# The end of the mixers in another order: one score level moved first, one branch's matmuls moved between the outputs of the linear attention, the output projection by halves of k

## The reference, cut to what matters

```
h = rms_norm(x);  proj = h @ w_in          # queries, keys, values of four mixers, and 4096 gate columns
y_nsa, y_sb, y_fox, y_gla                  # four mixers, 512 columns each; y_gla is the linear attention
branch = einsum('bsnc,ncd->bsnd', ys, w_branch)        # 4 products of 512 by 1024
mixed  = sum over n of sigmoid(gate_logits + b_gate)[n] * branch[n]
x = x + mixed @ w_out                      # 1024 by 1024
h2 = rms_norm(x);  x = x + relu(h2 @ w_ff1)**2 @ w_ff2
```

## Time and profile before

| | us |
|---|---|
| median of 3 runs | 1999.48 (1998.98 to 1999.66) |
| the profiled execution, its own time | 1997.83 |
| its span, first to last instruction | 1996.0 |
| PE busy | 1784.7 (89%) |
| DVE busy | 855.8 (43%) |
| ACT busy | 691.7 (35%) |
| POOL busy | 106.7 (5%) |
| mean granted TensorE clock | 0.950 |

### The profile page before, as it was taken

How to read it: one execution, slowest core, us unless ns; L and a number is a source line. 1 busy time by engine, 2 the same in 40 slices (tenths; PEclk the granted TensorE clock), 3 DMA queues, 4 the chain that set the end, 5 groups by cost and what they waited for, 6 DMA issues and landing times.

```text
span 1996.0 us, 27472 instructions
## 1 busy us (share of the span) xinstructions
PE 1784.7 (89%) x11676; PEld 1410.7 (71%) x11676; DVE 855.8 (43%) x1435; ACT 691.7 (35%) x1042; POOL 106.7 (5%) x112
## 2 busy tenths in 40 slices
PE   6987598899998869999997979998999989779997
PEld 4864443344443369889897879887889989769985
DVE  3033411111111154633476757535543446765643
ACT  1230211111111135654445334324555444534431
POOL 0000000000000001400200000000230110000000
PEclk9988699999999979999998989998999999889998
DMA  5422299999999845332422434534532333343451
GB/s 238 178 109 95 88 422 427 430 427 429 427 429 429 359 170 211 127 126 99 156 99 113 169 126 170 199 146 176 203 123 109 114 123 135 120 168 127 169 219 74
DMA packets 30872, 412.22 MB, mean 207 GB/s; under 512 B 3600, under 2 KB 5040, under 8 KB 5808
## 3 DMA queue, kind: packets, MB, share of 16 engines
q1 hardware_dynamic: 30768, 410.70, 51.5%
HBM read 408.85 MB, written 1.84 MB: 206 GB/s over the span
## 4 chain that ended last, share of the span: by engine, by line
PE 70%; issue 12%; DMA 9%; DVE 5%; ACT 2%; POOL 1%; SPq 0%; DVEq 0%; POOLq 0%; ACTq 0%
PE bank L1068 9%; PE bank L1069 9%; PE bank L1073 9%; DMA work_mem<-in_w 8%; PE bank L986 8%; PE bank L750 3%; PE bank L758 3%; PE bank L1003 3%; PE bank L1080 2%; PE bank L1081 2%; PE bank L1082 2%; PE bank L1090 2%; PE bank L1095 2%; PE bank L1091 2%; PE bank L1365 1%
## 5 line engine op out<-in xcount | busy, mean ns | idle before, releaser
L2190 DVE TENSOR_TENSOR w_lo<-wring,w_hi 128x2048 fp32r<-128x2048 f32 x88 | 201.3, 2292 | 186.4 <-ACT w_hi L1597 186.4
L1597 ACT ACTIVATE w_hi<-wring 128x2048 fp32r<-128x2048 f32 x88 | 168.6, 1916 | 301.8 <-PE bank L1069 168.3
L1068 PE MATMUL bank<-mixed_hi,w_hi_early 128*128 128x256 f32 x960 | 246.0, 293 | 7.0 <-DVE mixed_lo L2198 4.8
L1069 PE MATMUL bank<-mixed_lo,w_hi_early 128*128 128x256 f32 x960 | 240.5, 287 | 0.0
L1597 ACT ACTIVATE w_hi_early<-wring 128x2048 fp32r<-128x2048 f32 x80 | 152.9, 1911 | 231.5 <-PE bank L1069 154.5
L2190 DVE TENSOR_TENSOR w_lo<-wring,w_hi_early 128x2048 fp32r<-128x2048 f32 x80 | 182.5, 2286 | 90.1 <-ACT w_hi_early L1597 89.9
L1073 PE MATMUL bank<-mixed_hi,w_lo 128*128 128x256 f32 x1472 | 208.4, 285 | 0.0
L1068 PEld LDWEIGHTS bank<-mixed_hi,w_hi_early 128*128 128x128 f32 x960 | 187.8, 196 | 13.2 <-issue 8.1
L1073 PEld LDWEIGHTS bank<-mixed_hi,w_lo 128*128 128x128 f32 x1472 | 192.1, 194 | 0.0
L1069 PEld LDWEIGHTS bank<-mixed_lo,w_hi_early 128*128 128x128 f32 x960 | 188.2, 196 | 0.1
L986 PE MATMUL bank<-wring,gates_mem 128*64 128x512 f32 x768 | 168.3, 594 | 12.5 <-DMA wring<-in_w 12.5
(11 more groups left out here) (418 smaller groups left out, 3044.2 us busy)
## 6 DMA issues: line engine op xcount, KB each, us to landing
wring<-in_w SPq DMA_DIRECT2D x160, 2048.0 KB, 8.6
work_mem<-in_w SPq DMA_DIRECT2D x32, 2048.0 KB, 17.1
cst<-in_const SPq DMA_DIRECT2D x1, 1288.0 KB, 7.6
prm<-in_prm SPq DMA_DIRECT2D x3, 381.0 KB, 8.2
x_mem<-in_x SPq DMA_DIRECT2D x1, 1024.0 KB, 4.9
out_x<-x_mem SPq DMA_DIRECT2D x1, 1024.0 KB, 3.9
rel_skew<-work_mem SPq DMA_DIRECT2D x1, 768.0 KB, 3.6
work_mem<-in_prm SPq DMA_DIRECT2D x1, 512.0 KB, 12.6
```

The lines of the kernel that those rows point to most:

```text
L1068: pe.matmul(out, w[0][:, k, cols], x[0][:, k, :], start=(k == 0), stop=False)
L1069: mm = pe.matmul(out, w[0][:, k, cols], x[1][:, k, :], start=False, stop=False)
L1597: act.activation(hi, w, ACT.Copy).then_inc(hi_ready, 1)
L2190: dve.tensor_tensor(lo, w, hi, ALU.subtract).then_inc(lo_ready, 1)
```

## The change, and the diff

- **Levels.** `gla_steps` gives level 8 first, then 0 to 7, with the same eight gate products between. DVE reads level 8 in the step of level 0.
- **Halves.** The two-buffer part goes on for two halves more (`RINGED = LATE + 2`), so both halves of the first mixer's branch weight use `w_hi_early`.
- **ACT.** The sigmoid of the gate and `y_high(0)` move ahead of gate product 15, `y_high(1)` and `y_high(2)` follow level 7, and the gate sigmoids 0 to 3 are spread otherwise.
- **DVE.** `y_low(0)` moves ahead of the last level's reading, `y_low(1)` behind `var8`, `y_low(2)` behind `y_gla`, and the first four gated products are spread between them (`gated`).
- **PE.** The first branch's first product comes before `gla_o`, its other three between `gla_o` and `gla_t`; the banks follow (`plan_layer`).
- **Output projection.** All four column and row blocks with k tiles 0 to 3 first, then those with 4 to 7. The halves come as (26, first), (27, first), (26, second), (27, second) (`OUT_HALVES`). SP's table `uses` is not changed: chunk 26 is given free by `out` product 1, chunk 27 by `out` product 3.

```
+RINGED = LATE + 2
+OUT_HALVES = [(26, 0), (27, 0), (26, 1), (27, 1)]
...
-    for n in range(len(GLA_LEVELS) + 1):
+    for n in [levels] + list(range(levels)):
...
-    for name, count in (("gla_o", 2), ("gla_t", 2), ("branch", 16), ...
+    for name, count in (("branch", 1), ("gla_o", 2), ("branch", 3), ("gla_t", 2), ("branch", 12), ...
...
+        if 26 <= c < 28:
+            c, second = OUT_HALVES[h - (LATE + 8)]
...
 PE
+            branch(0, [0])
             in_sbuf(layer["gla_v"] + [j for n in range(9) for j in layer["gla", "level", n]], l, layer["gla_o"][0])
             for i, j in enumerate(layer["gla_o"]):
...
+            branch(0, [1, 2, 3])
             pe.wait_ge(y_gla, l + 1)
             for i, j in enumerate(layer["gla_t"]):
                 turn_four(j, o_g[:, i, :], l)
-            for n in range(N_BRANCH):
-                branch(n)
+            for br in range(1, N_BRANCH):
+                branch(br, range(4))
             for h in range(4):
-                half, second = divmod(h, 2)
+                second, half = divmod(h, 2)
                 w = half_ready(LATE + 8 + h)
-                pe.wait_ge(mixed_ready, 4 * l + (2 if h == 0 else 4))
+                pe.wait_ge(mixed_ready, 4 * l + (2 if second == 0 else 4))
...
 ACT
-                if h % 2 == 0:
+                if h % 2 == 0 or h == LATE + 9:
                     act.wait_ge(w_landed[c % RING], layer_landed(c, l))
...
+                elif n < last:
                     level(n + 1)
+                    if n == last - 1:
+                        act.activation(flat(sig_gg), flat(g_g), ACT.Sigmoid).then_inc(g_sig, 1)
+                        act.wait_ge(level_ready, 8 * l + last + 1)
+                        y_high(0)
+            full(layer["gla", "level", last][-1], l)
+            y_high(1)
+            y_high(2)
...
+            gate_sigmoid(0)
             (squares and copies of gla_o)
+            split_hi(RINGED + 0)
+            gate_sigmoid(1)
             act.wait_ge(var8_ready, l + 3)
+            split_hi(RINGED + 1)
+            gate_sigmoid(2)
             act.wait_ge(y_gla, l + 1)
+            split_hi(RINGED + 2)
...
 DVE
+            y_low(0)
+            level_read(levels - 1)
+            split_lo(LATE + 1)
             (silu and gain, sum of squares, var8)
+            y_low(1)
+            gated(0)
             dve.wait_ge(rstd8_ready, l + 3)
             then(dve.tensor_tensor(heads8(o_g), heads8(o_g), by_head(rstd8), ALU.mult))
             dve.tensor_tensor(o_g, o_g, sig_gg, ALU.mult).then_inc(y_gla, 1)
+            split_lo(RINGED + 0)
+            gated(1)
+            y_low(2)
+            gated(2)
+            split_lo(RINGED + 1)
+            gated(3)
             (low part of gla_t)
+            split_lo(RINGED + 2)
+            for n in range(4, 4 * N_BRANCH):
+                if n % 2 == 0:
+                    split_lo(LATE + n // 2 + AHEAD)
+                gated(n)
```

More of the change, by code:

```diff
@@ L340, in plan_layer @@
                 r.add((mixer, kind, n))
-    for name, count in (("gla_o", 2), ("gla_t", 2), ("branch", 16), ("out", 4), ("h2", 4), ("ff1", 16), ("ff2", 4)):
+    for name, count in (("branch", 1), ("gla_o", 2), ("branch", 3), ("gla_t", 2), ("branch", 12), ("out", 4), ("h2", 4), ("ff1", 16), ("ff2", 4)):
         r.add(name, count)
@@ L1368, in _, with branch @@
                                 mm.then_inc(bank_full[j.bank], 1)
+            def branch(br, ks):
+                pe.wait_ge(y_lo_ready, 5 * l + (br + 1 if br < 3 else 5))
+                tiles = slice(4 * br, 4 * br + 4)
+                for k in ks:
+                    w = half_ready(LATE + 2 * br + k // 2)
+                    split_a(layer["branch"][4 * br + k], w, 256 * (k % 2), (y_hi[:, tiles, :], y_lo[:, tiles, :]), k % 2 == 1)
+            branch(0, [0])
             in_sbuf(layer["gla_v"] + [j for n in range(9) for j in layer["gla", "level", n]], l, layer["gla_o"][0])
@@ L1591, in split_hi @@
                 c, w, hi, lo = weight_half(h)
-                if h % 2 == 0:
+                if h % 2 == 0 or h == LATE + 9:
                     act.wait_ge(w_landed[c % RING], layer_landed(c, l))
-                ahead, first = (2, 0) if h < LATE else (AHEAD, LATE)
+                ahead, first = (2, 0) if h < RINGED else (AHEAD, RINGED)
                 if h - first >= ahead:
@@ L1612, in next_hi @@
             def next_hi(h):
[L1613 removed]
+                if h + 2 < RINGED:
                     split_hi(h + 2)
@@ L1752, in _ @@
                     fill(*n)
-                else:
+                elif n < last:
                     level(n + 1)
-            for j in last_in_bank(layer["gla_g"] + layer["gates"]):
-                act.wait_ge(bank_read[j.bank], j.count(l))
[L1757 to L1764, removed]
+                    if n == last - 1:
+                        for j in last_in_bank(layer["gla_g"]):
+                            act.wait_ge(bank_read[j.bank], j.count(l))
+                        act.activation(flat(sig_gg), flat(g_g), ACT.Sigmoid).then_inc(g_sig, 1)
[4 more added lines that the diff above has]
+            y_high(2)
+            for j in last_in_bank(layer["gates"]):
+                act.wait_ge(bank_read[j.bank], j.count(l))
+            gate_sigmoid(0)
             for i, j in enumerate(layer["gla_o"]):
@@ L2410, in level_read @@
                     else:
-                        before = layer["gla", "level", n - 1][r]
-                        dve.wait_ge(bank_read[before.bank], before.count(l))
+                        if n < levels:
+                            before = layer["gla", "level", n - 1 if n > 1 else levels][r]
+                            dve.wait_ge(bank_read[before.bank], before.count(l))
                         apart()
@@ L2448, in _, with gated @@
                 dve.wait_ge(bank_read[j.bank], j.count(l))
[L2449 to L2453, removed]
-            for i, j in enumerate(layer["gla_t"]):
-                dve.wait_ge(y_hi_ready, 5 * l + 4 + i)
-                dve.tensor_tensor(y_lo[:, 12:16, i * P:(i + 1) * P], psum[j.bank][:, :].rearrange("p (h t) -> p h t", h=4),
-                                  y_hi[:, 12:16, i * P:(i + 1) * P], ALU.subtract).then_inc(bank_read[j.bank], 1)
-            for j in layer["gla_t"]:
-                dve.wait_ge(bank_read[j.bank], j.count(l))
-            dve.memset(mark, 0.0).then_inc(y_lo_ready, 2)
-            for n, j in enumerate(layer["branch"]):
+            def gated(n):
                 br, k = divmod(n, 4)
+                j = layer["branch"][n]
                 if n % 2 == 0:
-                    split_lo(LATE + n // 2 + AHEAD)
                     dve.wait_ge(gate_sig, 8 * l + n // 2 + 1)
```

60 lines of the change are left out of this document (36 added, 24 removed).

## The result

| | before | after |
|---|---|---|
| median of the runs on one chip, us | 1999.38 (1998.98 to 1999.66, 4 runs) | 1968.59 (1966.55 to 1973.02, 4 runs) |
| the profiled execution, its own time | 1997.83 | 1966.55 |
| its span | 1996.0 | 1964.7 |
| mean granted TensorE clock | 0.950 | 0.954 |

The ratio is 0.9849, with a 95% interval of 0.9837 to 0.9860: faster by 30.8 us. The forecast was 1968.9, and 1967.2 for the profiled execution.

The account below looks back on a forecast made before the run. PE (89% busy) bounds the kernel, with four holes a layer and low clock. Per layer -7.5 - 13.3 + 2.4 + 3.1 = -15.3, so -30.6 for two: 1999.5 becomes 1968.9 us, range 1961 to 1977.

Parts of the forecast that it names:

- Start of the levels: Forgetting mixer's end to gate product 15's end: 63.54 us becomes 56.1, 7.5 less a layer (4.8 idle, 2.7 clock).
- Level 7 to the end of the branches: PE's branch stage: 64.55 us becomes 51.3, 13.3 less a layer, with the holes of 1.59 and 9.66 covered.
- Output projection, its start: PE's hole before the output projection grows from 3.24 to 5.6 us by waiting for chunk 27: +2.4 a layer.
- Its end: Output projection's end: chunk 29 is issued a quarter later, so the norm comes 3.1 us later a layer.
- Clock behind the longer holes: PE's clock behind the two lengthened holes stays low as before: 0, bounds -1.7 and +1.7 us a layer.
- the four holes: PE's idle in each layer: 5.12 us before the first level, 1.59 before `gla_o`, 9.66 before `gla_t`, 3.24 before the output projection.
- (a): Rival, chance 0.13: before `gla_t` the chain to `y_gla` is not covered, 3 us a layer, 1974 to 1975.
- (b): Rival, chance 0.10: the two DMA waits cost little or PE's clock returns sooner, 4 to 5 us a layer less, 1959 to 1963.
- (c): Rival, chance 0.03: the branches run at 1.2 GHz, up to 46 us more in a layer, slower than before, 2060.
- (d): Rival, chance 0.02: PE stands before level 8 for something else and the middle gains little, 1996 to 2000.

Follow-up runs that it names:

- the first experiment: The kernel before with only the order of the levels changed (level 8 first): 1982.79 us, ratio 0.9912.
- the experiment on POOL alone: The changed kernel with `y_low(1)` moved on DVE from beside POOL's power to behind `y_gla`: 1968.91 us, ratio 0.9842.
- the longer chain: The changed kernel with POOL's power done twice, the first result unused, so that `y_gla` comes later: 1974.08 us, ratio 0.9868.
- the kernel with the weights by rows: The changed kernel with chunk 26 holding k tiles 0 to 3, chunk 27 those of 4 to 7, and chunk 26 freed by its own signal: 1955.94 us.

## Why the prediction was right

**Start of the levels.** Forecast 56.1 us from the forgetting mixer's end to the last level, measured 1050.39 - 994.60 = 55.8. PE needed no 0.3 for semaphores: level 8 starts without a hole behind the mixer's last product. Level 0's last multiply ends at 1000.86 (timeline of DVE, after), 0.7 before PE takes it at 1001.56, as the memset, decay and split of the earlier trace rows added up to. The clock stayed at 1.00, so the step that I had bounded by 4.8 to 7.8 came out near its upper end, 7.7, and the first experiment found the same amount alone.

**Level 7 to the end of the branches.** Forecast 51.3, measured 1050.39 to 1101.73 = 51.3. Timeline of DVE between them, after:

```profile
1062.16 1.23 DVE L2490 TENSOR_TENSOR work_mem<-work_mem,small 128x1024 f32<-128x1024 f32 x1 [0.93 <-POOL small L1846]
1063.42 1.23 DVE L2491 TENSOR_TENSOR work_mem<-work_mem 128x1024 f32<-128x1024 f32 x1
1064.56 2.29 DVE L2203 TENSOR_TENSOR w_lo<-wring,w_hi 128x2048 fp32r<-128x2048 f32 x1
```

`y_gla` ends at 1064.65 and PE's product 3 at 1065.77: 1.1 us of spare, 1.0 in the forecast. That is 14.26 after level 7's start, where my sum had 14.4. POOL took 2.58 and ended at 1062.13, 1.5 behind the end of `y_low(1)` at 1060.62, so it waited for it, or nearly; the sum had 12.0 on its own scale, and this is 11.7. The full 1.64 behind that end would give 1062.26. POOL was 0.13 sooner, and in the earlier trace rows it is 0.83 behind DVE's end where the pair alone takes 0.97: that 0.14 is too much for the rounding that the prediction called it. The low half for product 4 is written at 1066.85, so PE, which ends `gla_t` at 1066.81, goes on at 1066.95: 0.14, not 0.35. The Trainium skill (SBUF — State Buffer, Who interferes with whom) has a rule for this: a VectorE instruction with two SBUF inputs contends with a GpSimd instruction that reads SBUF, one with at most one does not. 2.58 against 1.64 agrees with it, and so does the gated product with its PSUM input, in the experiment on POOL alone, which lets POOL run at its 1.64. Moving `y_low(1)` out of POOL's way gained nothing, though: it only comes to stand ahead of the low half for product 4, and that kernel is as fast.

The drain that the Trainium skill (ScalarE: Activation LUTs, What ACT_TABLE_LOAD costs) adds to a table switch did not show: the load ahead of the sigmoid took its 1.28 with no idle time noted before it (timeline of ACT, after), and the 0.9 us a layer that this figure made of it are nowhere in PE's row.

```profile
1046.41 1.28 ACT L1773 ACT_TABLE_LOAD   x1
```

**Output projection, its start.** Forecast a hole of 5.6, measured 5.62 and 5.61. Timelines of SP, ACT and DVE, after, the two places where a load's landing decides:

```profile
1090.24 0.33 SPq L708 DMA_DIRECT2D wring<-in_w  x1
...
1097.91 1.91 ACT L1601 ACTIVATE w_hi<-wring 128x2048 fp32r<-128x2048 f32 x1 [5.22 <-DMA wring<-in_w]
1099.93 2.29 DVE L2203 TENSOR_TENSOR w_lo<-wring,w_hi 128x2048 fp32r<-128x2048 f32 x1 [3.21 <-ACT w_hi L1601]
...
1125.90 0.33 SPq L708 DMA_DIRECT2D wring<-in_w  x1
...
1133.72 1.91 ACT L1601 ACTIVATE w_hi<-wring 128x2048 fp32r<-128x2048 f32 x1 [6.81 <-DMA wring<-in_w]
1135.67 2.29 DVE L2203 TENSOR_TENSOR w_lo<-wring,w_hi 128x2048 fp32r<-128x2048 f32 x1 [6.43 <-ACT w_hi L1601]
1137.88 1.28 DVE L1887 TENSOR_TENSOR x_mem<-bank,x_mem 128x512 f32<-128x512 f32 x2
```

Chunk 27 is issued at 1090.24, 11.49 ahead of the branches' end (11.48 in the forecast), and ACT goes on 7.67 later, 3.8 ahead of that end. ACT had nothing to do for 5.22 us and DVE for 3.21, and from DVE's 1099.93 to PE's 1107.35 lie 7.42 us, the 7.4 of the earlier trace rows again.

**Its end.** Chunk 29 is issued at 1125.90 and ACT goes on at 1133.72, 2.4 behind PE's last product at 1131.3. The add to x, which needed only that product, starts at 1137.88 behind the split. Forecast +3.1, measured +3.2 in the first layer and +4.0 in the second. The second layer's lies near the far end of the bounds of 2.8 to 4.1: the same load took 8.6 us there.

**Clock behind the longer holes.** The term whose size was off: 0 in the forecast. In the output projection it was -0.8 and -0.9. The clock, granted at 0.50 from 1105 on, was back 4.0 us after PE's restart in the first layer and 3.8 in the second, where it took 5.9 (5.9 in the earlier trace rows) and 5.7 before. Behind the second longer hole, ahead of the feed-forward part, the prediction read no row. There it was +1.1 in the first layer and -1.45 in the second (the windows in the section on the result). The two together are +0.3 and -2.3 for a layer, against bounds of 1.7 either way, so the second layer lies outside them. Counting this clock the change brought -15.1 and -16.4 for twice -15.3. The remaining differences are in the landing, the levels, the 0.1 at `gla_t` and the 0.2 at product 4. What sets how soon the clock comes back stays open here: behind the same hole of 3.2 in one execution (old order of the projection, undone above) it took 3.0 in one layer and 6.2 in the other.

**Where luck helped.** The forecast for the median was 1968.9 and the median 1968.6. That is closer than the parts agree: the second layer's clock gave 2.3, its landing cost 0.9 more than forecast, and stretches that the change doesn't touch gave back some. The changed kernel's own runs lie over 6.5 us. The mechanism and the sizes of the four holes are borne out; the last 0.3 is luck.

**The rivals.** (a) fell with the 1.1 us of spare; the longer chain shows how near it was: behind the spare at `gla_t` stands a split that has none, so any longer chain is felt there. (b) fell as a whole and came true in a part: the landings were 7.7 to 8.6, and the clock gave 2.3 us in the second layer and cost 0.3 in the first, where (b) had 4 to 5 less in each. (c) fell: the clock is 1.00 in 1065 to 1070 and no hole is left ahead of the branches that could lower it. (d) fell: level 8 follows 0.34 us after the start of the product before it, and 5.1 us of hole are gone.

**What the prediction did not see** is that the order by k, which it rated as worth nothing and costing 5.5 us a layer, could keep its order without that cost, and that behind the old 9.4 lay 3.9 of a split that nobody needed so early.

## What to carry to other kernels

A wait for a DMA in an engine's in-order program costs what stands behind it, not what it waits for: here two splits for later products held up the gated products and the norm, and moving one of them behind the norm gave 14 us of 1969, of which the kernel before, with no landing to wait for, could have had 10. When the order of uses is changed, look at which buffer is then first wanted and which is last given free; the weights can be cut into chunks so that the two orders agree. A chain of short steps is best covered by products that don't need it, and a sum of such a chain row by row, with every instruction of the engine's program in it, was good to 0.2 us in 14.

## What the runs showed of the hardware

The power of 8 elements a partition on POOL took 1.64 us with DVE idle or beside a DVE instruction with one PSUM input, and 2.58 beside one with two SBUF inputs. The clock behind a hole of 5.6 us came back sooner than behind one of 3.2 at another time (4.0 us after PE's restart against 5.9), and behind two holes of 3.2 in one execution after 3.0 and 6.2. So the length of the hole does not set it alone. The loads of 2048 KB that PE's path waits for took 7.7 and 7.8 us in the first layer and 7.7 and 8.6 in the second. The changed kernel spread from 1966.55 to 1973.02, the one with the old order of the projection, which waits for no landing, from 1957.00 to 1958.05. That the landings make the spread is not shown: the kernel with the weights by rows waits for none either and spread over 4.4 us, and the time at the lower clock differs between executions too.
